# Four more taps of a depthwise convolution moved from TensorE to GpSimd, and VectorE's two taps moved one period later

## The chip, the cores and the metric

The kernel runs on one core of a Trainium2 chip. The metric is the device time of one execution in microseconds (us): the median of three runs. A profile of one execution, taken by the hardware profiler, stands beside it.

## The reference, cut to what matters

The program computes two transformer layers with 512 tokens and 1024 channels, and then two layers of another kind. The change touches the first stage of the first layer, a "conformer" convolution:

```python
def conformer_conv(x, pw1_w, pw1_b, dw_w, dw_b, ln_g, ln_b, pw2_w, pw2_b):
    h = x @ pw1_w + pw1_b                 # 1024 -> 2048
    a, g = jnp.split(h, 2, axis=-1)
    h = a * jax.nn.sigmoid(g)
    h = causal_dwconv(h, dw_w, dw_b)      # 31 taps, each channel by itself
    h = layer_norm(h, ln_g, ln_b)
    h = jax.nn.silu(h)
    return h @ pw2_w + pw2_b
```

`causal_dwconv` forms, for each channel, y[t] = b + sum over j = 0..30 of w[j] * x[t - 30 + j].

## The kernel before

Channels lie on the 128 partitions and the 512 tokens along the free dimension, so a tile of 128 x 512 float32 is one chunk of 128 channels; there are eight chunks (f = 0..7). Every matrix product is made of three TensorE products on operands split in a high and a low part: ScalarE (ACT) rounds a tile to its high part and VectorE (DVE) subtracts that to make the low part. This holds for the weights too: SyncE (SP) brings them in units of eight 128 x 128 blocks into three raw buffers, ACT writes `wh` (`round_to`), DVE writes `wl` (`rest_to`), both three units ahead of TensorE (PE), in a ring of four slots. In the steady part of the stage a period has three units.

The stage is a loop over chunks. Each engine's program is written out by hand, is executed in its own order, and the engines wait for one another on semaphores:

- PE: `pw1` of chunk f, 16 blocks (48 matmuls of 128 x 512), then `taps(f - 1)`. There one weight unit holds eight blocks `("dw", n, f)`; block n serves the taps 4n to 4n + 3 of the 32 positions (one is padding). A block is three rounds (high by high, low by high, high by low), each of four matmuls of 32 rows that run side by side in the four row groups of the array and write to the four banks 4 to 7. Block 0 (taps 1 to 3) isn't on PE at all. `taps(f)` waits for `c_lo` (the low part of the input tile `cin`), and for `c_sum` and `c_raw` (the banks have been read for the chunk before).
- ACT in iteration f: weight roundings, the sigmoid into `tmp`, `cinh` (high part of `cin`), then tap 1 as `Y = cin * coefficient + bias` (semaphore `c_base`), a square for the layer norm, and `conv_copy(f - 1)`: twelve copies of 32 rows out of the banks.
- DVE in iteration f: the low parts `wl` of the three units, `cin = (bank + bias) * sigmoid` (signals `c_glu`), `cinl` (signals `c_lo`), `first_taps(f)` (taps 2 and 3 as two `scalar_tensor_tensor` on `cin` and `Y`), `conv_stats(f - 2)` (two additions to the running sums), and `conv_sum(f - 1)`: four additions of 32 rows from the banks, then three of 128 rows of what ACT has copied.
- POOL (GpSimd) does nothing in this stage. Later it adds up `acc_s` for two layer norms.

After the loop stand `conv_sum(6)`, `conv_stats(5)`, `conv_sum(7)`, and then the layer norm. `cin`, `cinh` and `cinl` have two buffers each, so chunk f's are written anew for chunk f + 2.

Of the kernel before, what the change touches and what calls it, by code (L numbers as in the profile page):

```python
# [13 lines left out]
S = 512  # L14
# [10 lines left out]
PAD = TAPS  # L25
# [22 lines left out]
def weight_order():  # L48

    o = []  # L50

    def align():
        while len(o) % 4:
            o.append(None)

    o.extend(("pw1", k, c) for k in range(4) for c in FIRST)
    o.extend(("pw1", k, c) for f in range(2) for k in range(4, KD) for c in (f, 8 + f))
    o.extend([("dw", n, 0) for n in range(1, 8)] + [None])
    for f in range(2, 7):
        o.extend([("pw1", k, f) for k in range(KD)] + [("pw1", k, 8 + f) for k in range(KD)])  # L60
        o.extend([("dw", n, f - 1) for n in range(1, 8)] + [None])
    o.extend([("pw1", k, 7) for k in range(KD)] + [("pw1", k, 15) for k in range(KD)])
    for f in (6, 7):
        o.extend([("dw", n, f) for n in range(1, 8)] + [None])
    o += grouped("pp0", 2, list(range(8)), 1)
    o += grouped("pw2", KD, [0, 1, 2, 3], 4) + grouped("pw2", KD, [4, 5, 6, 7], 1)
    for layer in range(2):
        if layer == 1:
            o += [(mat, k, c) for k in range(KD) for mat in ("wq", "wk") for c in range(2)]
            for half in range(2):  # L70
                o += [("wv", k, 4 * half + c) for k in range(KD) for c in range(4)]
            for c in range(2, 8):
                o += [("wq", k, c) for k in range(KD)] + [("wk", k, c) for k in range(KD)]
            o += [("wo", k, c) for c in range(8) for k in range(5)]
            o += [("wo", k, c) for k in range(5, KD) for c in range(3)]
            o += [("wo", k, c) for c in range(3, 8) for k in range(5, KD)]
        if layer:
            o += grouped("pp1", 2, list(range(8)), 1)
        o += grouped(f"pg{layer}", KD, list(range(8)), 4)
        o += ffn_order(layer)  # L80
        o += grouped(f"down{layer}", FT, list(range(8)), 1)
    for layer in range(2):
        align()
        o += grouped(f"in{layer}", KD, list(range(4)), 4) + grouped(f"in{layer}", KD, [4, 5], 2)
        o += [(f"in{layer}", k, 8 + c) for k in range(KD) for c in range(4)]
        o += grouped(f"in{layer}", KD, [6, 7], 2)
        o += grouped(f"in{layer}", KD, list(range(12, 18)), 2)
        o += grouped(f"ukv{layer}", 1, list(range(4)), 4)
        o += grouped(f"uq{layer}", 2, [4, 5, 0, 1, 2, 3], 1)
        o += grouped(f"in{layer}", KD, [18, 19], 2)  # L90
        align()
        o += [(f"ukv{layer}", 0, 4 + c) for c in range(4)]
        for c in range(8):
            o += [(f"out{layer}", k, c) for k in range(4)]
        o += [(f"out{layer}", k, c) for c in range(4) for k in (4, 5)] + [(f"out{layer}", k, c) for k in (6, 7) for c in range(4)]
        o += [(f"out{layer}", k, c) for c in range(4, 8) for k in range(4, KD)]
    while len(o) % NU:
        o.append(None)
    return o


def param_order():
    o = [("b1", 16), ("dwb", 8), ("dwt", 24), ("lng", 8), ("lnb", 8), ("b2", 8)]
    for i in range(2):
        o += [(f"mixg{i}", 8), (f"mixb{i}", 8), (f"fcw{i}", 3 * FT), (f"fcb{i}", FT),
              (f"fg{i}", 8), (f"fb{i}", 8), (f"ng{i}", 8), (f"bgg{i}", 2), (f"glag{i}", 1),
              (f"mqg{i}", 2), (f"mkvg{i}", 1), (f"qgn{i}", 1), (f"qga{i}", 1), (f"qgb{i}", 1),
              (f"kgn{i}", 1), (f"kga{i}", 1), (f"kgb{i}", 1)]
    at, n = {}, 0
    for name, w in o:  # L110
        at[name] = n
        n += w
    return at, n
# [10 lines left out]
class Stream:  # L124


    def __init__(self):
        self.order = weight_order()
        self.units = len(self.order) // NU
        self.at = {}  # L130
        self.spare, self.slot, self.last_in = {}, {}, {}
        self.last = [0] * self.units
        for p, block in enumerate(self.order):
            if block is not None:
                self.at[block] = p
                self.last[p // NU] = p
        self.incs, self.total = [0] * len(self.order), []
        n = 0
        for p, block in enumerate(self.order):
            if block is not None:  # L140
                m, k, c = block
                ends = k == self.depth(m) - 1
                if self.by_token(m, c):
                    self.incs[p] = (4 if ends else int(self.last[p // NU] == p)) if c % 4 == 3 else 0
                else:
                    self.incs[p] = int(ends or self.last[p // NU] == p or (m, k) in HALVES)
            n += self.incs[p]
            self.total.append(n)
        for layer, mat in enumerate(("wq", "in0")):
            for e in range(3):  # L150
                self.spare[self.at[mat, 2 + 2 * e, 0] // NU] = (layer, e)
        for e, key in enumerate((("dw", 1, 6), ("dw", 1, 7), ("pp0", 0, 4), ("pw2", 0, 0))):
            self.spare[self.at[key] // NU] = (2, e)
        for e in range(4):
            self.spare[self.at["pg0", 2 * e, 0] // NU] = (3, e)
        ring = [u for u in range(self.units) if u not in self.spare]
        for n, u in enumerate(ring):
            self.slot[u] = n % SLOTS
            self.last_in[u] = ring[n - SLOTS] if n >= SLOTS else None
# [176 lines left out]
def place(nc, ctx, m):  # L336
# [6 lines left out]
    def ring(stack, name, n, shape, dt=F32):  # L343
        return [sb(stack, f"{name}{i}", shape, dt) for i in range(n)]
# [31 lines left out]
    with ExitStack() as ph:  # L376
        sb(ph, "conv_pp", [128, 4096])
        m.Y = sb(ph, "Y", [128, KD, S])
        sb(ph, "conv_pts", [128, 4096])
        m.taps2 = ring(ph, "taps2", 2, [128, S])  # L380
        m.cin = ring(ph, "cin", 2, [128, PAD + S])
        m.cinh = ring(ph, "cinh", 2, [128, PAD + S], FR)
        m.cinl = ring(ph, "cinl", 2, [128, PAD + S], FR)
    m.PP, m.HH, m.HL, m.pts = [], [], [], []
    for layer in range(2):
        with ExitStack() as ph:
# [162 lines left out]
def tensor_program(pe, m, s, w):  # L549
    X, XH, XL, bank, C = m.X, m.XH, m.XL, m.bank, m.C  # L550

    def mm(o, l, r, start, stop):
        return pe.e.matmul(o, l, r, start=start, stop=stop, skip_group_check=True)  # L553
# [189 lines left out]
    def taps(f):  # L743
# [5 lines left out]
        if f < 7:  # L749
            pe.wait_ge(s.c_sum, 4 * f)  # L750
            pe.wait_ge(s.c_raw, 12 * f)
        for n in range(1, 8):
            p = w.at["dw", n, f]
            u, j = p // NU, p % NU
            pe.wait_ge(s.w_lo, u)
# [3 lines left out]
            cols, tok = slice(j * 128, (j + 1) * 128), slice(4 * n + 3, 4 * n + 3 + S)  # L759
            for i in range(4):  # L760
                r = slice(32 * i, 32 * i + 32)
                mm(bank[b + i][:, :], h[r, cols], ch[r, tok], n == 1, False)
            for i in range(4):
                r = slice(32 * i, 32 * i + 32)
                mm(bank[b + i][:, :], h[r, cols], cl[r, tok], False, False)
# [546 lines left out]
def scalar_program(act, m, s, w, nc):  # L1312
    X, XH, bank, tmp, sqr, C, P = m.X, m.XH, m.bank, m.tmp, m.sqr, m.C, m.P

    def fn(o, i, f, **kw):
        return act.e.activation(o, i, f, **kw)  # L1316
# [163 lines left out]
    for f in range(8):  # L1480
# [2 lines left out]
        if f:  # L1483
            feed_group("pw1", range(KD), [8 + f])
        if 0 < f < 7:
            feed(("dw", 1, f - 1))
        if f == 7:
            round_to(w.at["pw2", 2, 0] // NU)
        act.wait_ge(s.stream, w.done("pw1", KD - 1, 8 + f))
# [8 lines left out]
        if f >= 2:  # L1498
            act.wait_ge(s.stream, w.done("dw", 7, f - 2))
        fn(m.cinh[f % 2][:, :], m.cin[f % 2][:, :], ACT.Copy).then_inc(s.c_hi, 1)  # L1500
        fn(m.Y[:, f, :], m.cin[f % 2][:, 1:S + 1], ACT.Identity, scale=P("dwt", 3 * f), bias=P("dwb", f)).then_inc(s.c_base, 1)
        if f == 4:
            embed_in(0)
        if f >= 2:
# [478 lines left out]
def vector_program(dve, m, s, w):  # L1983
# [252 lines left out]
    def first_taps(f):  # L2236
        y, ci = m.Y[:, f, :], m.cin[f % 2]
        dve.wait_ge(s.c_base, f + 1)
        n2 = dve.mark(stt(y, ci[:, 2:S + 2], P("dwt", 3 * f + 1), y, ALU.mult, ALU.add))
        dve.wait_ge(dve.own, n2)  # L2240
        tapped.append(dve.mark(stt(y, ci[:, 3:S + 3], P("dwt", 3 * f + 2), y, ALU.mult, ALU.add)))

    def conv_stats(c):
        if c:
# [5 lines left out]
    for f in range(8):  # L2250
# [2 lines left out]
        if f:  # L2253
            feed_group("pw1", range(KD), [8 + f])
        if 0 < f < 7:
            feed(("dw", 1, f - 1))
        if f == 7:
            rest_to(w.at["pw2", 0, 0] // NU)
        ci = m.cin[f % 2]
# [5 lines left out]
        stt(ci[:, PAD:], bank[2 * f % 4][:, :], P("b1", f), tmp[f % 2][:, :], ALU.add, ALU.mult).then_inc(s.c_glu, 1)  # L2265
        dve.wait_ge(s.c_hi, f + 1)
        less(m.cinl[f % 2][:, :], ci[:, :], m.cinh[f % 2][:, :]).then_inc(s.c_lo, 1)
        first_taps(f)
        if 2 <= f < 7:
            conv_stats(f - 2)  # L2270
        if f == 6:
            rest_to(w.at["pp0", 0, 0] // NU)
        if 0 < f < 7:
# [2 lines left out]
            embed_in(0)  # L2276
    conv_sum(6)
    conv_stats(5)
    conv_sum(7)
    rest_to(w.at["pw2", 4, 0] // NU)  # L2280
    variance_of(0, 0)
# [636 lines left out]
                    input_low(c - 1)  # L2918


def gpsimd_program(pool, m, s):
    C = m.C

    def tt(o, i0, i1, op):
        return pool.e.tensor_tensor(o, i0, i1, op)

    def add_sum(i, c, x0, x):
        pool.wait_ge(s.xsum, 8 * i + c + 1)
# [52 lines left out]
def lay_out(x):  # L2981
# [42 lines left out]

    put("b1", f["a_pw1_b"][0])
    put("dwb", f["a_dw_b"][0])
    put("dwt", np.ascontiguousarray(taps[1:4].reshape(3, 8, 128).transpose(1, 0, 2)))
    put("lng", f["a_ln_g"][0])
    put("lnb", f["a_ln_b"][0])
    put("b2", f["a_pw2_b"][0])  # L3030
# [74 lines left out]
```

## Time and profile before

| | before |
|---|---|
| median of 3 runs | 1749.47 us (1749.18 to 1750.5) |
| the profiled execution | 1748.82 us, span of its trace 1747.0 us |
| busy: PE, DVE, ACT, POOL | 1737.3, 1063.2, 847.0, 18.4 us |
| convolution loop | from 9 us to about 145 us of the span |

In the profile a row of the timeline is: start in us, duration in us, engine, line of the source, operation, output <- inputs, sizes, how many instructions are merged in it, and in brackets the idle time of the engine before it and what ended that. Durations overlap the next instruction of the same engine a little, so the distance from start to start is what one of a series costs. An instruction that is held up for a resource after it was issued shows as a longer one.

### The profile page before, as it was taken

To read this page: it belongs to the slowest core of one execution; us is meant where nothing else is said; L and a number is where in the kernel's file an instruction comes from. 1 tells how busy PE (TensorE), PEld (TensorE's weight loads), DVE (VectorE), ACT (ScalarE), POOL (GpSimd) and SP (SyncE) were. 2 spreads that over 40 slices of the span, in tenths; PEclk is the share of its full clock that TensorE was granted. 3 is DMA by queue.
4 is the path that set the end of the run, shared out by engine and by line. 5 is a ranking of instruction groups with operands and counts; after the bars stand their busy time and mean duration, and the time that the engine had idled before them with its cause. 6 is when DMAs were issued, how large, how long until landed. Compare 5 with 4: busy or idle time off the path is not lost.

```text
span 1747.0 us, 22538 instructions
## 1 busy us (share of the span) xinstructions
PE 1737.3 (99%) x9213; PEld 1409.8 (81%) x9213; DVE 1063.2 (61%) x1666; ACT 847.0 (48%) x1330; POOL 18.4 (1%) x21
## 2 busy tenths in 40 slices
PE   9999999999999999999999999999999999999999
PEld 7887988888888897777778888888898866778766
DVE  6788864444433465777784444443378866656674
ACT  7789643333332355666463333342255455534542
POOL 0000100000000000000200000000000000000000
PEclk9999999999999999999999999999999999999999
DMA  5331233322222222111132232223213221122111
GB/s 216 110 121 49 85 109 97 96 97 97 96 97 96 101 81 73 51 59 49 61 114 93 97 98 97 98 91 109 97 61 106 97 70 63 61 97 97 61 60 49
DMA packets 44679, 155.43 MB, mean 89 GB/s; under 512 B 5281, under 2 KB 5537, under 8 KB 44577
## 3 DMA queue, kind: packets, MB, share of 16 engines
q1 hardware_dynamic: 44576, 153.99, 26.1%
q8 instruction: 73, 1.20, 0.3%
q14 instruction: 30, 0.24, 0.0%
HBM read 149.78 MB, written 2.10 MB: 87 GB/s over the span
## 4 chain that ended last, share of the span: by engine, by line
PE 92%; DVE 4%; ACT 2%; issue 1%; DMA 0%; SPq 0%; DVEq 0%; ACTq 0%
PE bank L553 92%; ACT tmp L1316 1%; DVE tmp L1990 1%; PE bank L1261 0%; DVE sbl L1999 0%; DVE wl L1999 0%; DVE XL L1999 0%; DMA wraw<-in_wstream 0%; ACT taps L1316 0%; DVE acc_q L1987 0%; ACT wh L1316 0%; DVE HL L1999 0%; DVE sbh L2455 0%; DVE X L1987 0%; ACT XH L1316 0%
## 5 line engine op out<-in xcount | busy, mean ns | idle before, releaser
L553 PE MATMUL bank<-XH,wh 128*128 128x512 f32 (+1 forms) x1504 | 583.4, 388 | 3.2 <-DVE XL L1999 0.7
L553 PE MATMUL bank<-XH,wl 128*128 128x512 f32 (+1 forms) x1504 | 573.5, 382 | 0.0
L553 PE MATMUL bank<-XL,wh 128*128 128x512 f32 (+1 forms) x1504 | 573.5, 382 | 0.0
L1999 DVE TENSOR_TENSOR wl<-wraw,wh 128x1024 fp32r<-128x1024 f32 (+1 forms) x264 | 319.6, 1219 | 238.2 <-ACT wh L1316 237.6
L1316 ACT ACTIVATE wh<-wraw 128x1024 fp32r<-128x1024 f32 (+1 forms) x264 | 276.2, 1052 | 250.3 <-PE bank L553 243.7
L553 PEld LDWEIGHTS bank<-XH,wh 128*128 128x128 f32 x1504 | 282.8, 188 | 68.5 <-issue 8.9
L553 PEld LDWEIGHTS bank<-XH,wl 128*128 128x128 f32 x1504 | 282.8, 188 | 55.3
L553 PEld LDWEIGHTS bank<-XL,wh 128*128 128x128 f32 x1504 | 283.1, 188 | 52.3 <-issue 0.7
L1987 DVE SCALAR_TENSOR_TENSOR tmp<-bank,prm,tmp 128x511 f32<-128x511 f32 x88 | 65.9, 749 | 172.1 <-ACT tmp L1316 170.6
L553 PE MATMUL bank<-HH,wh 128*128 128x512 f32 (+1 forms) x420 | 155.8, 371 | 0.0
L553 PE MATMUL bank<-HH,wl 128*128 128x512 f32 (+1 forms) x420 | 154.1, 367 | 0.0
L553 PE MATMUL bank<-HL,wh 128*128 128x512 f32 (+1 forms) x420 | 154.0, 367 | 0.0
L1316 ACT ACTIVATE tmp<-bank,prm 128x512 f32<-128x512 f32 (+1 forms) x64 | 46.2, 723 | 193.0 <-PE bank L553 192.8
L1316 ACT ACTIVATE tmp<-tmp 128x512 f32<-128x512 f32 (+2 forms) x131 | 72.4, 596 | 86.3 <-DVE tmp L1987 85.8
L553 PEld LDWEIGHTS bank<-HH,wh 128*128 128x128 f32 x420 | 79.2, 189 | 13.8 <-DVE Y L1990 0.6
L553 PEld LDWEIGHTS bank<-HL,wh 128*128 128x128 f32 x420 | 79.2, 189 | 13.6 <-issue 0.5
L553 PEld LDWEIGHTS bank<-HH,wl 128*128 128x128 f32 x420 | 79.2, 189 | 12.9
L1316 ACT ACTIVATE tmp<-bank 128x512 f32<-128x512 f32 (+4 forms) x129 | 70.8, 567 | 17.8 <-PE bank L553 15.3
L1990 DVE TENSOR_TENSOR X<-X,bank 128x512 f32<-128x512 f32 (+1 forms) x58 | 38.4, 664 | 40.0 <-PE bank L553 40.0
L553 PE MATMUL bank<-XH,HL 128*128 128x256 f32 x256 | 57.4, 287 | 0.3 <-DVE XL L1999 0.2
L553 PE MATMUL bank<-wh,XH 128*128 128x512 f32 x128 | 50.7, 396 | 0.1
L553 PE MATMUL bank<-wh,XL 128*128 128x512 f32 x128 | 49.9, 390 | 0.0
(350 smaller groups left out, 2181.9 us busy)
## 6 DMA issues: line engine op xcount, KB each, us to landing
wraw<-in_wstream SPq DMA_DIRECT2D x276, 512.0 KB, 3.5
out<-X SPq DMA_DIRECT2D x8, 256.0 KB, 2.2
X<-in_xt SPq DMA_DIRECT2D x3, 512.0 KB, 8.5
pts<-in_pt SPq DMA_DIRECT2D x4, 256.0 KB, 4.1
eb<-lab SPq DMA_DIRECT2D x16, 64.0 KB, 2.0
cst<-in_consts SPq DMA_DIRECT2D x1, 810.5 KB, 9.9
X<-in_xt SPq DMA_DIRECT2D x2, 256.0 KB, 3.8
wraw<-in_wstream SPq DMA_DIRECT2D x2, 256.0 KB, 4.5
```

What stands on the lines that cost most here:

```text
L553: return pe.e.matmul(o, l, r, start=start, stop=stop, skip_group_check=True)
L1316: return act.e.activation(o, i, f, **kw)
L1987: return dve.e.scalar_tensor_tensor(out=o, in0=i0, scalar=sc, in1=i1, op0=op0, op1=op1)
L1990: return dve.e.tensor_tensor(o, i0, i1, op)
L1999: return dve.e.tensor_tensor(o, x, h.bitcast(F32), ALU.subtract)
```

## The change

- The `dw` block 1 (taps 4 to 7) of the chunks 0 to 6 is taken out of the weight stream (a hole of the same size stays) and out of `taps(f)` on PE, which begins with block 2 there. Chunk 7 keeps it.
- GpSimd makes these four taps for the chunks 0 to 6: for each tap a product `u = cin[shifted] * coefficient`, the coefficient being one column of the parameters spread over 512 elements, and after a wait for its own product, `Y = Y + u`. It starts chunk f when `c_base` says that ACT has written `Y`. That is eight `tensor_tensor` instructions of 128 x 512 for each chunk, 56 in all.
- DVE waits for GpSimd's eight instructions of chunk f before `first_taps(f)`, and does `first_taps(f - 1)` in iteration f, behind `conv_stats(f - 2)`; `first_taps(7)` stands behind `conv_stats(5)`, after the loop. Two buffers for the products and more columns of parameters (taps 1 to 7) are added.

```diff
 def weight_order():
-    o.extend([("dw", n, 0) for n in range(1, 8)] + [None])
+    o.extend([None] + [("dw", n, 0) for n in range(2, 8)] + [None])
     ...
 def taps(f):
-        for n in range(1, 8):
+        first = 2 if f < 7 else 1
+        for n in range(first, 8):
     ...
 def first_taps(f):
         y, ci = m.Y[:, f, :], m.cin[f % 2]
         dve.wait_ge(s.c_base, f + 1)
+        dve.wait_ge(s.pool, pool_taps(f + 1))
-        n2 = dve.mark(stt(y, ci[:, 2:S + 2], P("dwt", 3 * f + 1), y, ALU.mult, ALU.add))
+        n2 = dve.mark(stt(y, ci[:, 2:S + 2], P("dwt", 7 * f + 1), y, ALU.mult, ALU.add))
     ...
 (VectorE's loop)
         less(m.cinl[f % 2][:, :], ci[:, :], m.cinh[f % 2][:, :]).then_inc(s.c_lo, 1)
-        first_taps(f)
         if 2 <= f < 7:
             conv_stats(f - 2)
+        if f:
+            first_taps(f - 1)
     ...
     conv_sum(6)
     conv_stats(5)
+    first_taps(7)
     conv_sum(7)
     ...
+def pool_taps(f):
+    return 8 * min(f, 7)
+
 def gpsimd_program(pool, m, s):
+    for f in range(8):
+        y, ci = m.Y[:, f, :], m.cin[f % 2]
+        pool.wait_ge(s.c_base, f + 1)
+        for k in range(4, 8) if f < 7 else ():
+            u = m.taps_p[k % 2][:, :]
+            n = pool.mark(tt(u, ci[:, k:S + k], P("dwt", 7 * f + k - 1).broadcast_to([128, S]), ALU.mult))
+            pool.wait_ge(pool.own, n)
+            pool.mark(tt(y, y, u, ALU.add))
```

## Rows read from the trace of the kernel before

**Rows 1.** The chain that ended last: start us, length us, what.
```profile
9.05 121.31 PE bank L553 x945
130.37 0.59 ACT tmp L1316
...
144.53 0.70 DVE Y L1990
```
**Rows 2.** Stretch by engine: us, busy (x count), granted clock, DMA.
```profile
33.00:130.00 97.00, 97.00 (x800) 78.69 (x796) 75.47 (x98) 81.08 (x121) 0.00 (x0) 1.00 0.33 109
```
**Rows 3.** Timeline of VectorE over one period, from cinl of chunk 3 on.
```profile
64.49 0.72 DVE L1999 TENSOR_TENSOR cinl<-cin,cinh 128x543 fp32r<-128x543 f32 x1 [0.72 <-ACT cinh L1316]
65.20 1.54 DVE L1987 SCALAR_TENSOR_TENSOR Y<-cin,prm,Y 128x512 f32<-128x512 f32 x2
66.65 0.68 DVE L1990 TENSOR_TENSOR acc_s<-Y 128x512 f32<-128x512 f32 x1
67.97 2.80 DVE L1990 TENSOR_TENSOR Y<-Y,bank 32x509 f32<-32x509 f32 x4
70.80 0.69 DVE L1990 TENSOR_TENSOR Y<-Y,tmp 128x512 f32<-128x512 f32 x1
...
74.22 2.36 DVE L1999 TENSOR_TENSOR wl<-wraw,wh 128x1024 fp32r<-128x1024 f32 x2 [0.40 <-ACT wh L1316]
...
79.15 0.74 DVE L1987 SCALAR_TENSOR_TENSOR cin<-bank,prm,tmp 128x512 f32<-128x512 f32 x1
80.61 0.72 DVE L1999 TENSOR_TENSOR cinl<-cin,cinh 128x543 fp32r<-128x543 f32 x1 [0.72 <-ACT cinh L1316]
```
**Rows 4.** Timeline of PE in the taps of chunk 4 (block after block).
```profile
93.71 0.40 PE L553 MATMUL bank<-cinh,wh 32*128 32x512 f32 x4
...
94.40 0.41 PE L553 MATMUL bank<-cinh,wh 32*128 32x512 f32 x4
```
**Rows 5.** Timeline of ACT: where it waits for a DMA, before the last copies.
```profile
111.34 1.06 ACT L1316 ACTIVATE HH<-wraw 128x1024 fp32r<-128x1024 f32 x1 [1.49 <-DMA wraw<-in_wstream]
```
**Rows 6.** Timeline of GpSimd at its later additions, one instruction a row.
```profile
177.36 1.30 POOL L2925 TENSOR_TENSOR acc_s<-X 128x512 f32<-128x512 f32 x1 [176.93 <-DVE X L1987]
180.42 1.68 POOL L2925 TENSOR_TENSOR acc_s<-acc_s,X 128x512 f32<-128x512 f32 x1 [1.76 <-DVE X L1987]
182.73 1.68 POOL L2925 TENSOR_TENSOR acc_s<-acc_s,X 128x512 f32<-128x512 f32 x1 [0.63 <-DVE X L1987]
...
865.84 1.56 POOL L2925 TENSOR_TENSOR acc_s<-acc_s,X 128x512 f32<-128x512 f32 x1
867.54 1.56 POOL L2925 TENSOR_TENSOR acc_s<-acc_s,X 128x512 f32<-128x512 f32 x1
```
**Rows 7.** Timeline of VectorE at the same moments.
```profile
178.33 1.41 DVE L1999 TENSOR_TENSOR wl<-wraw,wh 128x1024 fp32r<-128x1024 f32 x1 [1.05 <-ACT wh L1316]
...
180.87 1.78 DVE L1987 SCALAR_TENSOR_TENSOR X<-X,tmp 128x512 f32<-128x512 f32 x1
182.57 0.68 DVE L1990 TENSOR_TENSOR acc_q<-acc_q,sqr 128x512 f32<-128x512 f32 x1
183.35 1.60 DVE L1990 TENSOR_TENSOR acc_q<-acc_q,sqr 128x512 f32<-128x512 f32 x1
...
868.46 0.69 DVE L1990 TENSOR_TENSOR X<-X,bank 128x512 f32<-128x512 f32 x1 [0.51 <-PE bank L553]
```
**Rows 8.** Timeline of VectorE at other chunks: 0, 2, 7, and the pts tiles.
```profile
26.59 0.72 DVE L1999 TENSOR_TENSOR cinl<-cin,cinh 128x543 fp32r<-128x543 f32 x1 [0.72 <-ACT cinh L1316]
...
28.76 2.35 DVE L1999 TENSOR_TENSOR wl<-wraw,wh 128x1024 fp32r<-128x1024 f32 x2
...
48.31 0.72 DVE L1999 TENSOR_TENSOR cinl<-cin,cinh 128x543 fp32r<-128x543 f32 x1 [0.72 <-ACT cinh L1316]
...
90.85 1.29 DVE L1999 TENSOR_TENSOR HL<-pts,HH 128x512 fp32r<-128x512 f32 x2
...
128.19 0.72 DVE L1999 TENSOR_TENSOR cinl<-cin,cinh 128x543 fp32r<-128x543 f32 x1 [1.22 <-ACT cinh L1316]
```

More of the change, by code:

```diff
@@ L57, in weight_order @@
     o.extend(("pw1", k, c) for f in range(2) for k in range(4, KD) for c in (f, 8 + f))
-    o.extend([("dw", n, 0) for n in range(1, 8)] + [None])
+    o.extend([None] + [("dw", n, 0) for n in range(2, 8)] + [None])
     for f in range(2, 7):
         o.extend([("pw1", k, f) for k in range(KD)] + [("pw1", k, 8 + f) for k in range(KD)])
-        o.extend([("dw", n, f - 1) for n in range(1, 8)] + [None])
+        o.extend([None] + [("dw", n, f - 1) for n in range(2, 8)] + [None])
     o.extend([("pw1", k, 7) for k in range(KD)] + [("pw1", k, 15) for k in range(KD)])
-    for f in (6, 7):
-        o.extend([("dw", n, f) for n in range(1, 8)] + [None])
+    o.extend([None] + [("dw", n, 6) for n in range(2, 8)] + [None])
+    o.extend([("dw", n, 7) for n in range(1, 8)] + [None])
     o += grouped("pp0", 2, list(range(8)), 1)
@@ L102, in param_order @@
 def param_order():
-    o = [("b1", 16), ("dwb", 8), ("dwt", 24), ("lng", 8), ("lnb", 8), ("b2", 8)]
+    o = [("b1", 16), ("dwb", 8), ("dwt", 56), ("lng", 8), ("lnb", 8), ("b2", 8)]
     for i in range(2):
@@ L151, in __init__ @@
                 self.spare[self.at[mat, 2 + 2 * e, 0] // NU] = (layer, e)
-        for e, key in enumerate((("dw", 1, 6), ("dw", 1, 7), ("pp0", 0, 4), ("pw2", 0, 0))):
+        for e, key in enumerate((("dw", 2, 6), ("dw", 2, 7), ("pp0", 0, 4), ("pw2", 0, 0))):
             self.spare[self.at[key] // NU] = (2, e)
@@ L383, in place @@
         m.cinl = ring(ph, "cinl", 2, [128, PAD + S], FR)
+        sb(ph, "conv_units", [128, 15 * S - 6 * (PAD + S + 1)])
+        m.taps_p = [sb(ph, "taps_p0", [128, S])]
+        sb(ph, "conv_emb", [128, 2 * S])
+        m.taps_p.append(sb(ph, "taps_p1", [128, S]))
     m.PP, m.HH, m.HL, m.pts = [], [], [], []
@@ L761, in taps @@
                 r = slice(32 * i, 32 * i + 32)
-                mm(bank[b + i][:, :], h[r, cols], ch[r, tok], n == 1, False)
+                mm(bank[b + i][:, :], h[r, cols], ch[r, tok], n == first, False)
             for i in range(4):
@@ L1485, in scalar_program @@
         if 0 < f < 7:
-            feed(("dw", 1, f - 1))
+            feed(("dw", 2, f - 1))
         if f == 7:
@@ L1500, in scalar_program @@
         fn(m.cinh[f % 2][:, :], m.cin[f % 2][:, :], ACT.Copy).then_inc(s.c_hi, 1)
-        fn(m.Y[:, f, :], m.cin[f % 2][:, 1:S + 1], ACT.Identity, scale=P("dwt", 3 * f), bias=P("dwb", f)).then_inc(s.c_base, 1)
+        fn(m.Y[:, f, :], m.cin[f % 2][:, 1:S + 1], ACT.Identity, scale=P("dwt", 7 * f), bias=P("dwb", f)).then_inc(s.c_base, 1)
         if f == 4:
@@ L2238, in first_taps @@
         dve.wait_ge(s.c_base, f + 1)
-        n2 = dve.mark(stt(y, ci[:, 2:S + 2], P("dwt", 3 * f + 1), y, ALU.mult, ALU.add))
+        dve.wait_ge(s.pool, pool_taps(f + 1))
+        n2 = dve.mark(stt(y, ci[:, 2:S + 2], P("dwt", 7 * f + 1), y, ALU.mult, ALU.add))
         dve.wait_ge(dve.own, n2)
-        tapped.append(dve.mark(stt(y, ci[:, 3:S + 3], P("dwt", 3 * f + 2), y, ALU.mult, ALU.add)))
+        tapped.append(dve.mark(stt(y, ci[:, 3:S + 3], P("dwt", 7 * f + 2), y, ALU.mult, ALU.add)))
     def conv_stats(c):
@@ L2255, in vector_program @@
         if 0 < f < 7:
-            feed(("dw", 1, f - 1))
+            feed(("dw", 2, f - 1))
         if f == 7:
@@ L2918, in vector_program @@
                     input_low(c - 1)
+def pool_taps(f):
+    return 8 * min(f, 7)
 def gpsimd_program(pool, m, s):
-    C = m.C
+    C, P = m.C, m.P
     def tt(o, i0, i1, op):
         return pool.e.tensor_tensor(o, i0, i1, op)
+    for f in range(8):
[6 more added lines that the diff above has]
+            pool.mark(tt(y, y, u, ALU.add))
     def add_sum(i, c, x0, x):
@@ L3026, in lay_out @@
     put("dwb", f["a_dw_b"][0])
-    put("dwt", np.ascontiguousarray(taps[1:4].reshape(3, 8, 128).transpose(1, 0, 2)))
+    put("dwt", np.ascontiguousarray(taps[1:8].reshape(7, 8, 128).transpose(1, 0, 2)))
     put("lng", f["a_ln_g"][0])
```

## The prediction

> **What bounds the kernel now.** I read the page first (PE busy 99% of the span), then the chain that ended last. In the convolution loop it is one unbroken piece of PE, 121.31 us from 9.05 on, to 130.37; from there to 145 it is ACT's copies and VectorE's last addition to `Y` [rows 1]. So until 130 whatever PE gives up could be a gain, and after it nothing of PE is. The stretch view says how much room the others have: in 97 us PE is busy 97.00, ACT 81.08, VectorE 75.47, GpSimd 0, at a granted clock of 1.00 [rows 2]. The timeline of VectorE then shows one period, from `cinl` of chunk 3 (64.49) to that of chunk 4 (80.61): 16.12 us [rows 3]. VectorE's own work in it, from start to start: two taps 1.45, two sums 1.3, bank additions 2.83, three additions of copies 3 x 0.7 = 2.1, three `wl` 3 x 1.17 = 3.5, `cin` 0.74, the round trip to ACT for `cinh` 0.72, `cinl` 0.71. The sum is 13.4, which leaves 2.8 us of idle time in a period of 16.1.
>
> **What PE gives up.** From 93.71 to 94.40 one `dw` block takes 0.69 us on PE [rows 4]; seven chunks give 7 x 0.69 = 4.8 us, and PE's period falls to 15.4. Not all of it could reach the end: ACT waits for a DMA of weights at 111.34 [rows 5], which hangs on a low part that VectorE made after ACT's copies of chunk 4, and from there ACT works without a pause up to 144.5. What stands ahead of that are four or five of the seven blocks, 2.8 to 3.4 us. The hole in the weight stream keeps the DMAs, roundings and units the same; the wider parameters (32 columns more) come while nothing waits for them: 0.
>
> **What GpSimd's eight instructions cost by themselves.** The trace has no product on GpSimd and no operand spread from one column. The nearest rows are additions of 128 x 512: 1.30 us where nothing disturbs it (177.36) and 1.56 to 1.68 elsewhere [rows 6]. From a first end, 865.84 + 1.56 = 867.40, to the next start at 867.54 a wait for its own result adds 0.14. So a chunk is 8 x 1.30 + 4 to 8 x 0.14 = 11.0 to 11.5 us, which would fit in 15.4. For the product I take 1.30 as for the addition; as bounds 0.7 (if the spread column costs half of the reading) and 1.9.
>
> **What they cost VectorE.** Here the rows speak against the change. GpSimd's addition at 182.73 ends at 184.41; VectorE's `acc_q` addition, issued at 183.35, takes 1.60 instead of 0.68 and ends at 184.95 [rows 6, 7]. The same at 180.42 (ends 182.10) against a `scalar_tensor_tensor` at 180.87 of 1.78 (ends 182.65), and at 177.36 (ends 178.66) against a `wl` at 178.33 (ends 179.74, 1.41 instead of 1.22). VectorE ends 0.55 after GpSimd (1.08 for the twice as long `wl`), which is its whole streaming time: it had not begun. The other way round, `acc_q` at 182.57 ends at 183.25 and GpSimd at 184.41, 1.16 later. So the two take turns, instruction by instruction, and while one reads the other stands. An addition with one operand in a bank isn't touched: 0.69 at 868.46 in the middle of GpSimd's 867.54 [rows 6, 7]. A turn of both is 1.15 + 0.55 = 1.70 us where VectorE alone needs 0.60: a GpSimd instruction that gets between two VectorE instructions of this kind costs VectorE 1.1 us.
>
> The Trainium skill has this as a rule: "SBUF — State Buffer", section "Who interferes with whom", says that a VectorE instruction with two SBUF inputs contends with a GpSimd instruction that reads SBUF, for a port pair held exclusively, and that the second one blocks fully. By that rule the offload isn't beside VectorE's work but in line with it, and these rows agree.
>
> In a period VectorE has ten such instructions (two taps, two sums, three additions of copies, three `wl`) and `cinl`; only `cin` and the four bank additions (3.5 us) are free of it. I walk a period from the end of `cinl`, when `c_base` lets GpSimd start. The four instructions of sums and taps let three of GpSimd's in (3 x 1.1). The four bank additions cover two more. Then the three additions of copies each wait for one of the last three (3 x 1.0 to 1.1). GpSimd ends about 13 us into the period, and the three `wl` are free. Period: 13.4 + 6 x 1.0 = 19.4 us (19.3 by the walk, instruction by instruction, which the sum uses) against 15.4 on PE and 16.1 before; VectorE becomes the bound. ACT's copies, done 9 us into the period, no longer end a wait.
>
> **The sum**, for the end of `cinl` of each chunk (before: 27.3, ..., 49.0 for chunk 2 [rows 8], 65.2, 81.3, ..., 128.9 for chunk 7 [rows 3, 8]):
> - Chunk 0 comes as before. GpSimd starts at 27.3 and needs 11.3 us plus turns for two `wl` (28.76 [rows 8]) and one `cinl`, 2: it ends at 40.6. Only then can VectorE do the taps of chunk 0, 7 us later than now.
> - From 40.6 to `cinl` of chunk 2: VectorE's work without sums 12.1, and six turns given (one between the taps, three at the copies, two at `wl`): 18.2. So 58.8 instead of 49.0.
> - Chunk 3 (no sums): 12.1 + 6.0, at 76.9. Chunk 4: +19.3, 96.2. Chunk 5: +19.3 and 1.2 for the `pts` parts [rows 8], 116.7. Chunk 6: +19.3, 136.0. Chunk 7: +19.3 and 1.1 for a fourth `wl`, 156.4, against 128.9 before: **27.5 us later**.
> - Behind that the loop's end goes as before, from `cinl` to `Y` at 144.53 [rows 1], but the taps of chunk 7 now stand inside it: +1.5 less about 0.5 of idle time there, +1.0.
> PE's 4.8 us are covered by its new waits. 1748.8 + 28.5 = 1777.3 for the profiled execution; the median is 0.65 above the profiled one, so 1778. I say 1777.
>
> **Rivals.**
> - *The product is cheap* (0.7 us). It blocks VectorE by 0.5 instead of 1.1; about three of the six turns in each period are products, and the opening is 2.4 us shorter: 6 periods x 1.8 + 2.4 = 13 us less, 1764.
> - *The product is dear* (1.9 us), or PE's waits, some 2 to 3 us twice in a period, bring the granted clock down from 1.00. The first adds 0.6 x 3 x 6 + 2.4 = 13 us: 1790. For the second: no row of the loop has PE waiting that long, so nothing there bounds it; if it made each period a microsecond longer it would be +6. Together up to 1796.
> - *The turns fall into VectorE's idle time*, PE stays the bound: **faster or equal**. Place: the additions of copies, where VectorE waits for ACT in any case, and its waits for `wh` and `cinh` (0.40 and 0.72 [rows 3]). It decides if the blocking adds under 15.4 - 13.4 = 2.0 us to a period, that is under two of the eight instructions meet one of VectorE's. The gain is then 2.8 to 3.4 minus 1.0 for the moved taps: 1747; with all 4.8 on the path 1745.7. Against it: right behind `c_base` four instructions of VectorE stand ready, so three turns are certain there, and the first chunk is late anyway.
> - *It doesn't do what it says*: the products fall behind `c_base` from chunk to chunk. Not by the sum: 13 us of a period of 19.
>
> **How the numbers follow.** Forecast 0.62 (own range 1768 to 1786), cheap product 0.13, dear product or clock 0.13, PE stays the bound 0.12, of which 0.05 is a gain of more than 0.2%. A difference of 0.2% (3.5 us) is about what a measurement of this kernel can tell from none. Faster 0.05, same 0.07, slower 0.88. The range for 8 in 10 reaches over the cheap and the dear product and leaves out the cases where PE stays the bound: 1758 to 1796.
>
> **What the profile would show.** Right: GpSimd 56 instructions more; VectorE's additions in SBUF at 1.6 to 1.8 us in the loop and those from banks still at 0.68; PE with waits of 2 to 3 us each period for `wl` and for VectorE's bank additions; distances of `cinl` of about 19 us; `cinl` of chunk 7 at about 156. Wrong: distances of 15.4 with PE unbroken (turns are free), products at 0.7 or 1.9 (mis-sized), PE at a clock under 1.00. The step I trust least is the product's duration, then that the two engines change turns after every single instruction.

## The result

The changed kernel takes 1773.71 us (median of four runs, 1773.43 to 1774.0) against 1749.33 us of the kernel before in the same session (1748.96 to 1750.5): a ratio of 1.0138, with a 95% interval of 1.0125 to 1.0151. It is 24.4 us slower; the forecast was 1777, 27.7 us slower.

The page of the changed kernel, busy time by engine and the shares of the chain that ended last:

```profile
span 1772.2 us, 22436 instructions
PE 1741.1 (98%) x9129; PEld 1414.1 (80%) x9129; DVE 1088.4 (61%) x1666; ACT 846.9 (48%) x1330; POOL 99.1 (6%) x77
PE 85%; DVE 9%; ACT 3%; issue 1%; DMA 1%; POOL 1%; SPq 0%; DVEq 0%; ACTq 0%
```

PE has 84 instructions less, POOL 56 more. DVE has the same 1666 instructions as before, and they are busy 25 us longer. In the chain that ended last its share has gone from 4% to 9%.

The timeline of VectorE over the period that answers to [rows 3], from `cinl` of chunk 3 to that of chunk 4:

```profile
71.91 0.72 DVE L2004 TENSOR_TENSOR cinl<-cin,cinh 128x543 fp32r<-128x543 f32 x1 [0.72 <-ACT cinh L1321]
72.55 0.68 DVE L1995 TENSOR_TENSOR acc_s<-Y 128x512 f32<-128x512 f32 x1
73.15 1.53 DVE L1995 TENSOR_TENSOR acc_q<-acc_q,sqr 128x512 f32<-128x512 f32 x1
74.60 1.77 DVE L1992 SCALAR_TENSOR_TENSOR Y<-cin,prm,Y 128x512 f32<-128x512 f32 x1
76.41 1.41 DVE L1992 SCALAR_TENSOR_TENSOR Y<-cin,prm,Y 128x512 f32<-128x512 f32 x1
77.92 2.79 DVE L1995 TENSOR_TENSOR Y<-Y,bank 32x509 f32<-32x509 f32 x4
80.75 1.14 DVE L1995 TENSOR_TENSOR Y<-Y,tmp 128x512 f32<-128x512 f32 x1
82.00 1.34 DVE L1995 TENSOR_TENSOR Y<-Y,taps 128x511 f32<-128x511 f32 x1
83.44 1.59 DVE L1995 TENSOR_TENSOR Y<-Y,tmp 128x510 f32<-128x510 f32 x1
84.96 3.48 DVE L2004 TENSOR_TENSOR wl<-wraw,wh 128x1024 fp32r<-128x1024 f32 x3
88.37 0.74 DVE L1992 SCALAR_TENSOR_TENSOR cin<-bank,prm,tmp 128x512 f32<-128x512 f32 x1
89.83 0.72 DVE L2004 TENSOR_TENSOR cinl<-cin,cinh 128x543 fp32r<-128x543 f32 x1 [0.72 <-ACT cinh L1321]
```

And GpSimd's timeline in it:

```profile
72.66 1.47 POOL L2937 TENSOR_TENSOR taps_p<-cin,prm 128x512 f32<-128x512 f32 x1 [6.09 <-ACT Y L1321]
74.21 1.61 POOL L2937 TENSOR_TENSOR Y<-Y,taps_p 128x512 f32<-128x512 f32 x1
75.78 1.49 POOL L2937 TENSOR_TENSOR taps_p<-cin,prm 128x512 f32<-128x512 f32 x1
77.35 1.62 POOL L2937 TENSOR_TENSOR Y<-Y,taps_p 128x512 f32<-128x512 f32 x1
78.93 1.03 POOL L2937 TENSOR_TENSOR taps_p<-cin,prm 128x512 f32<-128x512 f32 x1
80.04 1.30 POOL L2937 TENSOR_TENSOR Y<-Y,taps_p 128x512 f32<-128x512 f32 x1
81.29 1.50 POOL L2937 TENSOR_TENSOR taps_p<-cin,prm 128x512 f32<-128x512 f32 x1
82.87 1.62 POOL L2937 TENSOR_TENSOR Y<-Y,taps_p 128x512 f32<-128x512 f32 x1
```

Read the two side by side. Each engine's instruction ends a fixed time after the other's: the product ends at 74.13 and `acc_q` at 74.68; the addition at 75.82 and the first tap at 76.37, 0.55 later each time. In the other direction `acc_s` ends at 73.23 and the product 0.90 later, `acc_q` at 74.68 and the addition 1.14 later. During the four bank additions (77.92 to 80.71) the product at 78.93 and the addition at 80.04 have their undisturbed 1.03 and 1.30. What the six held-up instructions of VectorE take over their time in the kernel before is 0.85 + 1.02 + 0.66 + 0.45 + 0.65 + 0.90 = 4.5 us, and 13.4 + 4.5 = 17.9 us is the distance from 72.63 to 90.55. Apart from the 0.72 us for `cinh`, as before, VectorE waits for nothing in this period.

The distance from the end of `cinl` of one chunk to the next, from the timeline's `cinl` rows of each kernel (the kernels of the experiments are described below), in us. `cinl` of chunk 0 itself ends between 27.3 and 29.0 us in these traces, so a difference of a few tenths in the first column, and of up to 1.7 us for e2_free, is that late start and not a gain:

| to chunk | 2, from 0 | 3 | 4 | 5 | 6 | 7 | 0 to 7 |
|---|---|---|---|---|---|---|---|
| before | 21.7 | 16.2 | 16.1 | 16.3 | 16.0 | 15.2 | 101.6 |
| forecast of the change | 31.5 | 18.1 | 19.3 | 20.5 | 19.3 | 20.4 | 129.1 |
| changed kernel | 27.5 | 17.4 | 17.9 | 19.3 | 21.9 | 21.1 | 125.1 |
| e1_feed | 28.7 | 16.8 | 17.9 | 19.3 | 19.4 | 19.4 | 121.4 |
| e2_free | 19.5 | 15.4 | 15.5 | 16.3 | 18.8 | 15.6 | 101.1 |
| e3_free_feed | 21.0 | 15.5 | 15.5 | 16.3 | 16.1 | 15.2 | 99.6 |
| e4_reads | 28.0 | 16.9 | 18.2 | 19.4 | 21.0 | 19.6 | 123.1 |
| e5_writes | 26.3 | 14.6 | 14.8 | 16.3 | 16.1 | 15.2 | 103.3 |
| e6_half | 21.0 | 15.4 | 15.7 | 17.1 | 17.1 | 17.6 | 104.0 |
| e7_late_start | 22.4 | 16.8 | 17.9 | 19.3 | 19.4 | 19.4 | 115.1 |
| e8_block_alone | 21.0 | 15.5 | 15.5 | 16.3 | 16.0 | 15.2 | 99.5 |
| e9_sparse | 21.8 | 15.4 | 16.7 | 16.3 | 16.1 | 15.2 | 101.5 |

In the changed kernel the last column is 23.5 us more than before, and from `cinl` of chunk 7 to the end of VectorE's last addition to `Y` it is 17.7 us instead of 16.3: 24.9 us, against the 24.4 measured.

The periods to chunks 6 and 7 are longer than turns alone make them, though. The timeline of ACT and of VectorE at chunk 6, and below it VectorE's row at the same chunk in the kernel before:

```profile
128.06 1.06 ACT L1321 ACTIVATE HH<-wraw 128x1024 fp32r<-128x1024 f32 x1 [6.20 <-DMA wraw<-in_wstream]
129.33 1.06 ACT L1321 ACTIVATE HH<-wraw 128x1024 fp32r<-128x1024 f32 x1 [0.21 <-DMA wraw<-in_wstream]
130.97 0.73 DVE L2004 TENSOR_TENSOR cinl<-cin,cinh 128x543 fp32r<-128x543 f32 x1 [4.65 <-ACT cinh L1321]
```
```profile
112.97 0.72 DVE L1999 TENSOR_TENSOR cinl<-cin,cinh 128x543 fp32r<-128x543 f32 x1 [2.21 <-ACT cinh L1316]
```

ACT waits for the DMA, `cinh` stands behind it, and VectorE waits 4.65 us instead of 2.21. (ACT's own wait, 1.49 us before [rows 5] and 6.20 now, isn't the measure: with the feeding mended, in e1_feed, it is still 5.52 us, as ACT now comes to it early, and VectorE's is 2.25.) The code has the reason, and the prediction had overlooked it. `feed` makes weights three units ahead only if the block it is given stands at the first place of its unit. The hole shifted block 2 to the second place, so `feed(("dw", 2, f - 1))` does nothing, on ACT and on VectorE, and every third unit is made one feeding later. At chunk 7 VectorE so has a unit more to make low in its period (five instead of four), beside GpSimd's reads. PE shows the late weights early in the loop; PE's timeline there, and three stretches of the view by stretches (the third number from the end of a line is the granted clock):

```profile
50.98 0.80 PE L557 MATMUL bank<-cinh,wh 32*128 32x512 f32 x4 [6.78 <-DVE wl L2004]
51.54 0.66 PE L557 MATMUL bank<-cinl,wh 32*128 32x512 f32 x4
51.97 0.66 PE L557 MATMUL bank<-cinh,wl 32*128 32x512 f32 x4
...
56.58 0.41 PE L557 MATMUL bank<-cinl,wh 32*128 32x512 f32 x4
56.81 0.41 PE L557 MATMUL bank<-cinh,wl 32*128 32x512 f32 x4
```
```profile
48.00:50.00 2.00, 0.00 (x0) 0.00 (x0) 2.00 (x2) 0.00 (x0) 1.67 (x2) 0.50 0.00 0
50.00:54.00 4.00, 3.02 (x28) 2.69 (x32) 3.77 (x4) 0.20 (x1) 0.00 (x0) 0.50 0.54 136
54.00:58.00 4.00, 4.00 (x49) 3.18 (x46) 2.85 (x4) 1.73 (x4) 2.69 (x2) 0.69 0.69 257
```

PE stands for 6.78 us; within that wait its granted clock falls to 0.50, the level of 1.2 GHz, and stays there at first when PE goes on: a round of taps takes 0.43 us from start to start until 56.2 and 0.23 after it.

### The profile page after: what moved, and what is told of

Read it like the earlier page. It is cut to its first block, busy times and chain, and to the rows that moved or that the text cites. A ratio compares the mean times of both kernels' runs of the same rounds, so it can differ in the third digit from the quotient of the medians.

```text
span 1772.2 us, 22436 instructions
## 1 busy us (share of the span) xinstructions
PE 1741.1 (98%) x9129; PEld 1414.1 (80%) x9129; DVE 1088.4 (61%) x1666; ACT 846.9 (48%) x1330; POOL 99.1 (6%) x77
## 4 chain that ended last, share of the span: by engine, by line
PE 85%; DVE 9%; ACT 3%; issue 1%; DMA 1%; POOL 1%; SPq 0%; DVEq 0%; ACTq 0%
PE bank L557 85%; DVE Y L1995 2%; DVE wl L2004 1%; ACT tmp L1321 1%; DVE Y L1992 1%; DVE tmp L1995 1%; DMA wraw<-in_wstream 1%; PE bank L1266 0%; DVE sbl L2004 0%; DVE HL L2004 0%; ACT taps L1321 0%; POOL Y L2937 0%; DVE XL L2004 0%; ACT Y L1321 0%; DVE acc_q L1995 0%
## 5 line engine op out<-in xcount | busy, mean ns | idle before, releaser
L1995 DVE TENSOR_TENSOR X<-X,bank 128x512 f32<-128x512 f32 (+1 forms) x58 | 38.5, 666 | 40.0 <-PE bank L557 40.0
```

What stands on the lines that cost most here:

```text
L1995: return dve.e.tensor_tensor(o, i0, i1, op)
```

## The experiments

**The theory** was that the turns VectorE and GpSimd take at SBUF cost most of the time. **The rivals** were the late weights, the waits for GpSimd's result, and the moved taps. Each diff shows the main edit alone, against the changed kernel where nothing else is said; counts to wait for, tiles and names that go with it are left out. From e3_free_feed on the feeding is mended in every variant of the changed kernel.

**e1_feed**: the unit is fed at its old place.

```diff
-            feed(("dw", 2, f - 1))
+            round_to(w.at["dw", 2, f - 1] // NU + AHEAD)     # ACT; rest_to on VectorE
```

> The changed kernel with one thing mended: in it block 2 of a dw unit no longer stands at the first place of its unit, so the line that feeds this unit (only a block at a first place triggers the making of weights three units ahead) does nothing, on ACT and on VectorE, and every unit of weights is made one unit later than before. Here the unit is fed again at its old place. Theory A (VectorE's turns with GpSimd set the period, the late weights cost only where another engine is seen waiting): VectorE's idle time at chunk 2 (0.62 + 1.41 + 1.04 us for PE and ACT) goes, and of its 4.65 us at chunk 6 (ACT waits for a DMA of weights) about 3 us go; total 1773.7 - 5 = 1768 to 1770 us, distances of cinl at chunks 3 to 5 as in the changed kernel (17.4 to 19.3). Theory B (the late weights are the main cause): back to within 3 us of 1749.

Measured: 1770.48 us, before 1749.8, ratio 1.0117 (1.0100 to 1.0134). Of 24.4 us, 20.7 stay. So the late weights are a real part, some 3.7 us (3.2 between the two medians themselves), and not the main one. By the table the gain lies in chunks 3, 6 and 7 (0.6 + 2.4 + 1.7 us), while the opening is 1.1 us longer, since a unit more gives turns there. It came out 0.5 us over the range I had given.

**e2_free** and **e3_free_feed**: GpSimd's instructions and VectorE's wait for them are taken away, with the feeding as in the change and mended.

```diff
-        dve.wait_ge(s.pool, pool_taps(f + 1))
-    (GpSimd's loop of 56 instructions)
```

> The changed kernel without GpSimd's 56 instructions and without VectorE's wait for them (taps 4 to 7 of the first seven chunks are left out of the result); the hole in the weights, the late feeding and the moved taps stay. Theory A (GpSimd's reads cost VectorE some 4 to 6 us a period): PE sets the period again, distances of cinl about 15.5 us, total 1746 to 1750 us, so 24 to 28 us under the changed kernel. Theory B (late weights): still over 1760. Theory C (the moved taps of VectorE): still over 1755.

Measured: 1750.93 us, before 1749.8, ratio 1.0006 (0.9996 to 1.0015). That is 0.9 us over the theory's upper end; both rivals' numbers (over 1755, over 1760) are out.

> As e2_free, with the unit of weights fed at its old place. This is what the removal of the block from PE would bring if GpSimd's work were free. Theory A: seven blocks are 4.8 us, of which ACT's chain behind chunk 5 lets 2.8 to 3.4 through, and the moved taps take 1.0 to 1.4 back: 1746.5 to 1748 us. If ACT's chain is not what limits it: 1749.3 - 4.8 + 1.4 = 1745.9.

Measured: 1748.9 us, before 1749.8, ratio 0.9997 (0.9987 to 1.0006), 0.9 us over the upper bound. With GpSimd's work for nothing, the change gives 0.9 us, which can't be told from none. The loop is 2.0 us shorter (101.6 to 99.6), not 2.8 to 3.4, and 1.4 of it go to the moved taps. The timelines of ACT and of VectorE in its period to chunk 5, in which nothing is gained:

```profile
79.70 1.14 ACT L1321 ACTIVATE HH<-pts 128x512 fp32r<-128x512 f32 x2
...
86.31 2.43 ACT L1321 ACTIVATE tmp<-bank 32x510 f32<-32x510 f32 x4
```
```profile
88.77 0.69 DVE L1995 TENSOR_TENSOR Y<-Y,tmp 128x510 f32<-128x510 f32 x1 [0.82 <-ACT tmp L1321]
89.38 1.29 DVE L2004 TENSOR_TENSOR HL<-pts,HH 128x512 fp32r<-128x512 f32 x2
90.58 3.49 DVE L2004 TENSOR_TENSOR wl<-wraw,wh 128x1024 fp32r<-128x1024 f32 x3
93.99 0.75 DVE L1992 SCALAR_TENSOR_TENSOR cin<-bank,prm,tmp 128x512 f32<-128x512 f32 x1
```

**e4_reads**: the kernel before with all its work, and 56 instructions of GpSimd for which nobody waits.

```diff
+    for f in range(7):
+        pool.wait_ge(s.c_base, f + 1)
+        for k in range(4):
+            n = pool.mark(tt(m.taps_p[0][:, :], m.cst[:, 0:S], m.cst[:, k:k + 1].broadcast_to([128, S]), ALU.mult))
+            pool.wait_ge(pool.own, n)
+            n = pool.mark(tt(m.taps_p[1][:, :], m.cst[:, S:2 * S], m.taps_p[0][:, :], ALU.add))
+            pool.wait_ge(pool.own, n)
```

(The diff is against the kernel before.)

> The kernel before, whose whole work stays, and beside it GpSimd's 56 instructions in the loop on tiles of their own (products of a constant tile with a spread column, additions of two tiles), started at the same signal for which nobody waits. It prices the reading alone. Theory A: VectorE's additions in SBUF grow to 1.3 to 1.7 us, six turns of about 0.9 us a period minus 2.8 us of idle time, some 2 to 2.5 us for each of chunks 2 to 7 and a little more where VectorE held up ACT's copies: +10 to +16 us, 1759 to 1765. Theory B (waits for GpSimd's result, not its reads, cost the time): within 2 us of 1749.

Measured: 1770.88 us, before 1749.8, ratio 1.012 (1.0105 to 1.0135): **21.1 us for GpSimd's instructions beside the others**, with PE's work unchanged, nobody waiting for GpSimd and no data shared with it. These instructions read and write; which of the two it is, e5_writes tells. The direction is the theory's, the size is 5 to 6 us over its range. VectorE's timeline shows where I had counted too little:

```profile
65.58 5.42 DVE L2003 TENSOR_TENSOR wl<-wraw,wh 128x1024 fp32r<-128x1024 f32 x3
...
73.09 2.20 DVE L1991 SCALAR_TENSOR_TENSOR Y<-cin,prm,Y 128x512 f32<-128x512 f32 x2
75.21 1.77 DVE L1994 TENSOR_TENSOR acc_s<-Y 128x512 f32<-128x512 f32 x1
76.91 1.52 DVE L1994 TENSOR_TENSOR acc_q<-acc_q,sqr 128x512 f32<-128x512 f32 x1
78.46 2.80 DVE L1994 TENSOR_TENSOR Y<-Y,bank 32x509 f32<-32x509 f32 x4
```

Where GpSimd is behind, its last instructions meet the `wl` too (5.42 us for three instead of 3.5), and the opening costs 6.3 us, which I had called "a little more". Once more the four bank additions take 2.80.

**e5_writes**: e1_feed, with three memsets for each of GpSimd's instructions.

```diff
-            n = pool.mark(tt(u, ci[:, k:S + k], P("dwt", 7 * f + k - 1).broadcast_to([128, S]), ALU.mult))
-            pool.wait_ge(pool.own, n)
-            pool.mark(tt(y, y, u, ALU.add))
+            for i in range(6):
+                n = pool.mark(pool.e.memset(u, 0.0))
+                pool.wait_ge(pool.own, n)
```

> e1_feed with each of GpSimd's two instructions for a tap replaced by three memsets of a 128 x 512 tile of its own, each waiting for the one before, so that GpSimd only writes (taps 4 to 7 of the first seven chunks are left out of the result); VectorE waits for it as before. If a memset takes 0.45 to 0.55 us, GpSimd is busy some 12 to 15 us a chunk, as long as with the true work. Theory A (its reads of SBUF hold VectorE up, neither its activity nor the waiting for it): VectorE's additions stay at 0.68 us, distances of cinl 15.5 to 16.3 us from chunk 3 on; a late start of chunk 0's taps (about 6 us of waiting) costs at most 3 us at the end: 1749 to 1752 us. Theory B (writes hold it up as well, or the waits do): 1760 to 1770 us.

Measured: 1753.16 us, before 1749.52, ratio 1.0020 (1.0010 to 1.0029), 1.2 us over the theory's range and well under the rival's. GpSimd's group of instructions, and VectorE's timeline in the period to chunk 4:

```profile
L2945 POOL MEMSET taps_p<- 128x512 f32 x168 | 88.5, 527 | 40.7 <-ACT Y L1321 31.2
```
```profile
68.35 0.68 DVE L1995 TENSOR_TENSOR acc_s<-Y 128x512 f32<-128x512 f32 x1
68.96 0.68 DVE L1995 TENSOR_TENSOR acc_q<-acc_q,sqr 128x512 f32<-128x512 f32 x1
69.64 1.54 DVE L1992 SCALAR_TENSOR_TENSOR Y<-cin,prm,Y 128x512 f32<-128x512 f32 x2
71.29 2.80 DVE L1995 TENSOR_TENSOR Y<-Y,bank 32x509 f32<-32x509 f32 x4
74.12 0.69 DVE L1995 TENSOR_TENSOR Y<-Y,tmp 128x512 f32<-128x512 f32 x1
```

GpSimd is busier than in the change (88.5 us against 81.5 in the loop), VectorE waits for it as there, and not one of these instructions is longer than before. So it is the reads that hold VectorE up. What the waits cost by themselves is the 4.3 us against e3_free_feed (the two were measured in different sessions): VectorE stands 8.5 us for chunk 0 and 1.7 us for chunk 1, and part of that is caught up in chunks 3 and 4 (14.6 and 14.8 us). I had allowed 3 us for it.

**e6_half**: e1_feed with the products alone.

```diff
             pool.wait_ge(pool.own, n)
-            pool.mark(tt(y, y, u, ALU.add))
```

> e1_feed with the four products of each chunk and without the four additions (taps 4 to 7 of the first seven chunks are left out of the result). A smaller dose of reads: four instructions of 1.04 us. Theory A: in a period three of them meet one of VectorE's (sums and taps) for 0.85 us each and the fourth lies beside the bank additions: 13.4 + 2.6 = 16.0 us of VectorE's time against 15.4 of TensorE's, so distances of 15.9 to 16.5; total 1749 + 6 x 0.5 = 1750 to 1754 us. The cost isn't half of the 21 us, since the idle time of VectorE swallows the first 2 us of each period. If the cost went with the number of instructions alone: 1748.9 + 10.8 = 1759.7.

Measured: 1752.9 us, before 1749.52, ratio 1.0019 (1.0009 to 1.0028), within the theory's range. Half of the instructions cost 4.0 us over e3_free_feed, all of them 21.6 (e1_feed). The distances to chunks 3 and 4 (15.4 and 15.7) are nearly those without GpSimd, as VectorE's idle time takes in the three turns. At chunks 5 to 7, where it has little or none that could take them in, each period is 0.7 to 2.4 us longer.

**e7_late_start**: e1_feed with chunk 0 left whole on PE, GpSimd on chunks 1 to 6.

> e1_feed with the taps 4 to 7 of chunk 0 left on TensorE (GpSimd serves the chunks 1 to 6). Theory: the opening, in which VectorE waits 4.7 to 6.0 us for GpSimd and gives turns to two units of weights, cost about 7 us in the distance from cinl of chunk 0 to that of chunk 2 (28.7 in e1_feed against 21.7 before), and 0.7 us of TensorE's saving is given up, which isn't on the path: 1770.5 - 6 = 1763 to 1766 us. Rival (the opening is absorbed later by slack): no change, 1770.

```diff
-    o.extend([None] + [("dw", n, 0) for n in range(2, 8)] + [None])
+    o.extend([("dw", n, 0) for n in range(1, 8)] + [None])
```

Measured: 1765.4 us, before 1749.52, ratio 1.0086 (1.0071 to 1.0101). The opening is 22.4 us instead of 28.7, and all later distances are the same to 0.03 us: while VectorE is the bound, what it loses early isn't given back. Chunk 0 alone costs 5.1 us of the total (6.3 in the loop; about 1 us of it is taken in behind the loop, where VectorE waits for others), as its period is the shortest: `cinl` of chunk 1 comes 5.9 us after that of chunk 0.

**e8_block_alone**: the kernel before without the block on PE for chunks 0 to 6, and nothing instead.

```diff
-            first_taps(f - 1)        # VectorE's taps at their old place, in iteration f
+            first_taps(f)
-    (GpSimd's loop, VectorE's wait for it)
```

> The kernel before with the block of taps 4 to 7 of the first seven chunks taken out of the weights and of TensorE and nothing in its place (these taps are left out of the result): no GpSimd, VectorE's taps at their old place, the weights fed at their old place. It is the most that the offload could give. Theory: of seven blocks (4.8 us) only the 2.0 us reach the end that e3_free_feed shows between cinl of chunk 0 and of chunk 7, since VectorE is full at chunk 5 and ACT waits for a DMA at chunk 6; the 1.4 us of the moved taps don't fall due: 1747.0 to 1748.0 us. If the moved taps cost nothing at the end: 1748.9 as e3_free_feed.

(The diff is against the changed kernel.) Measured: 1747.12 us, before 1749.55, ratio 0.9987 (0.9978 to 0.9996). It is the ceiling of the offload: 2.4 us, by the interval 0.7 to 3.8. From `cinl` of chunk 7 to the last addition to `Y` it is 16.3 us, as before, and in e3_free_feed 17.7, as in the change; so the moved taps cost 1.4 us, as the traces have it; in the medians it is 1.5, less than the intervals can resolve.

**e9_sparse**: GpSimd on the chunks 1 and 3 only, the taps of the others where they were.

```diff
+POOLED = (1, 3,)
-        for k in range(4, 8) if f < 7 else ():
+        for k in range(4, 8) if f in POOLED else ():
```

> GpSimd makes the taps 4 to 7 for the chunks 1 and 3 only, and only these two have their VectorE taps a period later; weights fed at their old place; the rest is as in the kernel before. Theory: a period with GpSimd's eight instructions takes VectorE 17.9 us where 15.4 are there, the next one without them gives 2 us back, and since the weights are made a unit and more ahead TensorE doesn't stand: two blocks, 1.4 us, are gained and the end is unmoved: 1748.0 us, 1747.5 to 1749. Rival (each period with GpSimd costs its 2 to 2.5 us at the end, whatever follows): 1752 to 1754 us.

Measured: 1749.37 us, before 1749.55, ratio 0.9999 (0.9990 to 1.0008). The rival is out: two chunks of GpSimd's work don't cost 2 us each at the end. The gain of 1.4 us doesn't show either; the interval (1.7 us faster to 1.4 slower) can't exclude it, but the trace has it gone. VectorE's timeline in the period to chunk 4, and its first row in the next:

```profile
72.62 1.32 DVE L2005 TENSOR_TENSOR Y<-Y,tmp 128x510 f32<-128x510 f32 x1 [0.38 <-ACT tmp L1331]
73.87 5.42 DVE L2014 TENSOR_TENSOR wl<-wraw,wh 128x1024 fp32r<-128x1024 f32 x3
...
81.39 1.54 DVE L2002 SCALAR_TENSOR_TENSOR Y<-cin,prm,Y 128x512 f32<-128x512 f32 x2
```

The turns at the `wl` (5.42 us for three) make that period 16.7 where it is 15.5 without GpSimd: the 0.7 us won up to chunk 3 are down to 0.1 by chunk 4. The next period has four taps (its own and the late ones) and takes 16.3, as in every kernel without GpSimd's reads there, so it gives nothing back. No version tried with GpSimd beats the kernel before.

## Why the prediction was right, point by point

- **The bound passes to VectorE by turns at SBUF**: right, and shown: GpSimd's instructions beside unchanged work cost 21.1 us (e4), the same waiting with writes only leaves VectorE's instructions as they were (e5), and the rows of both engines interlock to a hundredth. The rule of the Trainium skill ("SBUF — State Buffer", section "Who interferes with whom") holds here in both its halves: reads contend, writes alone don't.
- **The price of a turn**: nearly right where GpSimd's instruction is an addition: a turn of both is 1.14 + 0.55 = 1.69 us (forecast 1.70), and the two such turns of the period shown cost VectorE 1.02 and 0.90 us (forecast 1.0 to 1.1). The product was mis-sized: 1.04 us undisturbed instead of 1.30, and its three turns 0.85, 0.66 and 0.65 instead of 1.1. The first of the three additions of copies lost 0.45, not 1.0, since GpSimd was further on. So a period came to 17.9 us instead of 19.3, and with 4 us from the opening the loop up to chunk 5 was 7 us too long in the forecast.
- **"The hole in the weight stream keeps the DMAs, roundings and units the same"**: wrong. The hole took away what triggers the feeding. I read the change of `feed` as a new name for the same unit, and not what `feed` tests. Price 3.7 us (e1), in chunks 6 and 7 above all. It has the opposite sign to the error before, and without it the change would have come out at about 1770, 7 us under the forecast. That the point estimate missed by 3 us only was luck: two errors met. The range would have held either way.
- **The opening**: GpSimd is done with chunk 0 at 38.5 us (forecast 40.6), and VectorE waits 5.98 us for it; the distance to chunk 2 is 27.5 us, forecast 31.5. That it isn't caught up later is right (e7).
- **PE's 4.8 us don't reach the end**: right. But the part that could, 2.8 to 3.4 us, was too high by the traces: 2.0 and 2.1 us in the loop (e3, e8), and ACT's wait for the DMA at chunk 6 ends at 109.9 us in e3_free_feed instead of 111.3. The medians (2.4 us in e8, interval 0.7 to 3.8) can't decide this. The step that failed: I saw ACT's wait at chunk 6 and not that ACT and VectorE by themselves fill the period to chunk 5, even before. Its distance is 16.3 us in every kernel without GpSimd's reads, with the block on PE or without it. The rows of e3_free_feed above show why: ACT rounds the `pts` tiles ahead of its twelve copies, and VectorE does its last addition, its `pts` parts, three `wl` and `cin` behind the last copy without a pause.
- **The moved taps**: +1.0 forecast, +1.4 measured (17.7 against 16.3, e3 against e8).
- **The rival with PE's clock**: the clock fell to 0.50 in the 6.78 us wait, a longer wait than the 2 to 3 us I had counted with (those came too: 1.84, 2.23 and 2.39 us at the taps of chunks 3 to 5). Much of it came from the late feeding: with it mended PE waits 1.63 and 1.90 us there. It made the taps of chunk 1 some 2.7 us longer (6.8 us, from 50.98 to 57.83, instead of 18 rounds of 0.23, 4.1), at a place where VectorE then waited for ACT and PE for 3.1 us. Behind it VectorE is the bound again. The mean clock is under 1.00 later on too (0.91 from 80 to 100 us, 0.88 from 130 to 150), but from chunk 3 to the loop's end VectorE waits for no bank of PE's. In e4_reads 6.3 us were lost up to chunk 2 with a granted clock of 1.00 from 20 to 60 us, and in e7_late_start the period to chunk 3 is 16.8 us, as in e1_feed, with 1.00 from 20 to 80. So the clock isn't the cause.
- **The rival in which idle time takes in the turns**: its threshold (2.0 us a period) fits what was measured. With the products alone the periods to chunks 3 and 4 are within 0.2 us of those without GpSimd (e6), with all eight instructions they are 1.3 and 2.4 us over (e1).

What stays open is how the two engines' turns would go with longer instructions, and whether another order of VectorE's work (its bank additions right behind `c_base`, where they don't contend) would hide enough of GpSimd's work to gain the 2.4 us; it wasn't tried.

## What to carry to other kernels

An idle engine isn't always free capacity: before work goes to GpSimd, count VectorE's instructions with two SBUF inputs in the same period, since each instruction of GpSimd that reads SBUF stands in line with them, and compare the sum with VectorE's idle time, not with GpSimd's. Measure first what the removal alone brings (here about 2.4 us of 4.8), as the price has to stay under that. And when an item leaves a list whose positions trigger something, look for what was triggered by its place.

## What the runs showed of the hardware

A GpSimd product of a 128 x 512 tile with a column spread over 512 elements takes 1.04 us undisturbed, an addition of two tiles 1.30 us; a memset of that size 0.53 us. Between GpSimd's reads and VectorE's instructions with two SBUF inputs the turns change after every single instruction, and both pay: GpSimd's addition grows to 1.62 us, and VectorE's of 0.68 us to between 1.34 and 1.78 us. VectorE's `cin`, which reads a bank and one tile, keeps its 0.74 us, and its bank additions theirs; beside memsets of GpSimd none is longer. In a wait of 6.78 us the clock granted to PE fell to 0.50, and PE then ran for about 5.2 us at this lower level, with 0.43 instead of 0.23 us a round.
